# Expert weights in 2 MB pairs: the down pairs issued by ScalarE's queue instead of SyncE's

## What is computed

```python
# grouped_moe, for each of the two layers
scores = sigmoid(t @ router_w)             # 256 tokens x 16 experts
# two experts per token, both inside the best group of four
for e in range(16):
    h = silu(t @ w_gate[e]) * (t @ w_up[e])    # 2048 -> 512, twice
    y = y + combine[:, e:e+1] * (h @ w_down[e])  # 512 -> 2048
x = layer_norm(ALPHA * x + y)
```

## Time and profile before

| | us |
|---|---|
| median of three runs | 1601.77 (1600.47 to 1601.79) |
| profiled execution, its own time | 1603.34 |
| its span, first to last instruction | 1601.4 |
| PE busy | 1539.1 (96%) |
| DVE busy | 699.7 (44%) |
| ACT busy | 453.5 (28%) |
| DMA engines, share of the span that SyncE's queue fills | 79.9% |

### The profile page before, as it was taken

How to read it: one execution, slowest core, us unless ns; L and a number is a source line. 1 busy time by engine, 2 the same in 40 slices (tenths; PEclk the granted TensorE clock), 3 DMA queues, 4 the chain that set the end, 5 groups by cost and what they waited for, 6 DMA issues and landing times.

```text
span 1601.4 us, 18456 instructions
## 1 busy us (share of the span) xinstructions
PE 1539.1 (96%) x7630; PEld 901.7 (56%) x7630; DVE 699.7 (44%) x1010; ACT 453.5 (28%) x600; POOL 9.5 (1%) x19
## 2 busy tenths in 40 slices
PE   9999999999999999899889999999999999999994
PEld 7888887885343343343338888888534335334332
DVE  5544567645333332332247474463543233233325
ACT  5334466434010111011036463342411102111102
POOL 0010000000000000000000000000000000000000
PEclk9999999999999999999999999999999999999998
DMA  8655333578999999999997555457899999999996
GB/s 329 249 194 210 106 132 141 203 280 332 397 428 428 427 427 427 429 426 430 423 414 303 184 200 185 157 203 281 320 424 426 429 426 427 427 428 428 428 422 245
DMA packets 50886, 527.47 MB, mean 329 GB/s; under 512 B 5579, under 2 KB 5643, under 8 KB 12530
## 3 DMA queue, kind: packets, MB, share of 16 engines
q1 hardware_dynamic: 49586, 522.27, 79.9%
q0 software_dynamic: 1216, 4.02, 0.8%
HBM read 524.17 MB, written 2.10 MB: 329 GB/s over the span
## 4 chain that ended last, share of the span: by engine, by line
PE 79%; DMA 16%; DVE 2%; ACT 1%; SPq 1%; issue 0%; DVEq 0%; ACTq 0%
PE bank L1361 29%; DMA w_all<-in_moe_w_down 11%; PE bank L867 10%; PE bank L869 10%; PE bank L868 10%; PE bank L1319 4%; PE bank L1429 3%; DMA router_pair<-in_moe_w_down 2%; DMA w_all<-in_moe_w_gate_up 2%; PE bank L1444 1%; PE bank L1519 1%; DMA w_land<-in_ev_w_in 1%; PE bank L1332 1%; PE bank L1412 1%; PE bank L879 1%; PE bank L931 1%
## 5 line engine op out<-in xcount | busy, mean ns | idle before, releaser
L1361 PE MATMUL bank<-w_all,xg 128*64 128x512 f32 x1856 | 414.4, 596 | 13.1 <-DMA w_all<-in_moe_w_gate_up 11.9
L867 PE MATMUL bank<-w_hi,T_hi 128*128 128x512 f32 x736 | 290.4, 395 | 2.9 <-DVE w_lo L2260 1.4
L869 PE MATMUL bank<-w_hi,T_lo 128*128 128x512 f32 x736 | 286.8, 390 | 0.0
L868 PE MATMUL bank<-w_lo,T_hi 128*128 128x512 f32 x736 | 286.5, 389 | 0.0
L2184 DVE TENSOR_TENSOR w_lo<-w_land,w_hi 128x2048 fp32r<-128x2048 f32 x90 | 205.0, 2289 | 177.6 <-ACT w_hi L1719 177.4
L1361 PEld LDWEIGHTS bank<-w_all,xg 128*64 128x64 f32 x1856 | 127.8, 137 | 268.3 <-issue 241.5
L1719 ACT CAST w_hi<-w_land 128x2048 fp32r<-128x2048 f32 x94 | 178.1, 1911 | 217.9 <-PE bank L869 215.8
L2745 DVE TENSOR_TENSOR y_lo<-bank,y_hi 128x512 fp32r<-128x512 f32 x54 | 37.4, 692 | 415.0 <-ACT y_hi L1980 415.0
L2756 DVE SCALAR_TENSOR_TENSOR X<-bank,weight,X 128x512 f32<-128x512 f32 x224 | 152.5, 744 | 49.6 <-PE bank L1429 49.6
L867 PEld LDWEIGHTS bank<-w_hi,T_hi 128*128 128x128 f32 x736 | 138.2, 188 | 35.2 <-issue 4.3
L869 PEld LDWEIGHTS bank<-w_hi,T_lo 128*128 128x128 f32 x736 | 138.2, 188 | 29.2
(11 more groups left out here) (376 smaller groups left out, 1399.5 us busy)
## 6 DMA issues: line engine op xcount, KB each, us to landing
w_all<-in_moe_w_gate_up SPq DMA_DIRECT2D x114, 2048.0 KB, 20.9
w_all<-in_moe_w_down SPq DMA_DIRECT2D x50, 2048.0 KB, 21.4
w_land<-in_od_w_in SPq DMA_DIRECT2D x32, 1024.0 KB, 4.9
w_land<-in_ev_w_in SPq DMA_DIRECT2D x31, 1024.0 KB, 4.9
router_pair<-in_moe_w_gate_up SPq DMA_DIRECT2D x10, 2048.0 KB, 17.4
w_land<-in_ev_w_out SPq DMA_DIRECT2D x16, 1024.0 KB, 4.8
w_land<-in_od_w_out SPq DMA_DIRECT2D x16, 1024.0 KB, 4.8
router_pair<-in_moe_w_down SPq DMA_DIRECT2D x6, 2048.0 KB, 22.6
```

What stands on the lines that cost most here:

```text
L867: pe.matmul(dst, hi_l, hi_r, start=start, stop=False)
L868: pe.matmul(dst, hi_l, lo_r, start=False, stop=False)
L869: return pe.matmul(dst, lo_l, hi_r, start=False, stop=stop)
L1361: ins = pe.matmul(dst[halves[h], :], cols(c), U.weights(q, pos + h)[:, c, :], start=start and c == 0, stop=stop and c == 3)
```

## The change

ScalarE issues the down pairs. The function `fetch_down(e)` stands in ScalarE's stream right behind `silu(e)` and issues the two down pairs of expert e there (one for expert 0, whose first down pair is among the nine early ones). It waits for the same `used` count as before. In layer 1, from expert 4 on, it reads the expert's number from SBUF, as SyncE did four at a time. SyncE keeps the gate/up pairs, the nine early pairs and the four blocks at the end of a layer. Places, sizes, the order in which TensorE uses the pairs, and all arithmetic stay.

```diff
-                    def down(pos, e):
-                        for p in range(1 if first and e == 0 else 0, 2):
-                            fetch(pos + 2 * p, e, 1, p)
-
                     for e in range(4):
                         up_gate(12 * e, e)
-                        if (e or not first) and not (last and e == 3):
-                            down(12 * e + 8, e - 1)
...
                     def down(pos, e, following):
                         y_out(pos, e, 0)
                         silu(following)
+                        if not (last and following >= 2):
+                            fetch_down(following)
                         if last and following == 2:
                             slots_pair()
                         else:
...
+                    def fetch_down(e):
+                        at_e = 4 * q + e
+                        if layer and at_e >= 4:
+                            act.wait_ge(flag_ready, layer + 1)
+                            number = act.value_load(number_of[0:1, at_e:at_e + 1], min_val=0, max_val=NEXP - 1)
+                        else:
+                            number = at_e
+                        for p in range(1 if at_e == 0 else 0, 2):
+                            n = U.number(q, 12 * e + 20 + 2 * p)
+                            act.wait_ge(used, U.freed(n))
+                            act.dma_start(pair_at(U.place(n)).rearrange("p u n -> p (u n)"),
+                                          moe_src(layer, number, 1, p)).then_inc(pair_in[U.place(n)], 16)
...
                             slots(0)
                             silu(0)
+                            fetch_down(0)
                             continue
```

## The result

The changed kernel takes **1630.74 us** (median of four runs, 1626.64 to 1633.43); the kernel before took 1601.78 beside it (1600.47 to 1603.91). The ratio is 1.0175 with a 95% interval of 1.0163 to 1.0187: slower by 29 us, between 26 and 30. The forecast was 1628, the range 1611 to 1643. The profiled execution of after took 1633.43 us with a span of 1631.5, against 1603.34 and 1601.4.

What follows compares the result with a forecast made beforehand. The prediction took DMA transfers at 428 GB/s, slower than PE, to bound the experts; terms A to D, 12.4 + 8.6 + 3.5 + 1.7 = 26.2 us, added to the 1601.77 median gave 1628 us, range 1611 to 1643.

Steps and rivals of the forecast that it cites:

- What bounds the kernel, and what is removed: Expert stages: transfers at 428 GB/s are slower than PE; no gate/up pair can start earlier, so the gain is zero at best.
- ScalarE's cost at 0: Behind silu: the added issues and read, 0.7 to 1.5 us per expert, are hidden and cost 0.
- Term A: Start of each layer: down pairs issued later leave DMA engines idle, 6.2 us a layer, 12.4 in all.
- No further idle: After a layer's start: later down pairs are delayed less, other transfers stay in flight, so no more DMA time is lost.
- Term B: End of each layer: down pairs overtake the last gate/up pairs, so PE ends it 4.3 us later, 8.6 in all.
- Term C: Layer 1's wide expert 8: PE's release comes later relative to the transfers, 3.5 us of idle DMA; bounds 0 and 6.4.
- Term D: Last wait of each layer: TensorE's clock falls to half behind longer PE waits; one fall, 1.7 us, bounds 0 to 3.4.
- Service transfer by transfer: Rival on both queues: served in order of issue, nothing overtakes and only the layer-start loss stays, 1614 us; 15%.
- a loss or a gain of rate: Two rivals while both queues are active: they move less together, 1635 to 1647 us, 13%; or more, 1598 us, 6%.
- longer and rarer: Sign to look for: PE's waits for gate/up pairs become longer and fewer, in front of j = 2 and 3.

Runs made afterwards that it cites:

- e5: Against the kernel before: SyncE still issues every pair, but each down pair waits for its expert's silu, placed in PE's order of use; 1617.22 us.
- e6: Changed kernel with down pairs of experts 0, 1 and 13 of both layers, and 5 and 6 of layer 1, back on SyncE's queue; 1604.54 us.
- e9: The changed kernel measured once more, without an edit, for a comparison on one chip; 1630.31 us.
- e8: Changed kernel with only the down pairs of experts 5 and 6 of layer 1, ahead of the wide expert, back on SyncE's queue; 1625.92 us.
- e3: Changed kernel with the down pairs of experts 0 and 1 of each layer back on SyncE, issued as early as before; 1622.95 us.
- e10: Changed kernel with eight filler matmuls of 128 x 256 ahead of the fourth gate/up pair of expert 14; 1627.52 us.

## Why the prediction was right, step by step

**What bounds the kernel, and what is removed: held.** SyncE's first gate/up issue behind the nine early pairs stands at 390.57 in after and at 390.35 in the earlier trace rows. Counted from layer 0's first gather, its 65 gate/up issues come 0.0 to 15.9 us later than before, none earlier; no gate/up pair gained from the freed queue. The sentence of the Trainium skill that the prediction set against the change, on the page "DMA: Bandwidth & Descriptors", section "Issuing engines are not separate DMA queues", agrees with the plateaus at 427 to 428 GB/s. About half of the loss was made by the order of landing: e5, with the lateness alone, is 15.1 us over before, after 29.0.

**ScalarE's cost at 0: held where it was looked for.** Two issues take 0.8 us behind silu, and e6, with 20 experts' issues still on ScalarE, is 2.4 us over before in all, which bounds it.

**Term A: 6.2 us a layer, measured 6.4 in layer 0.** The gap at 386 is there, the issue at 410, and the short gap announced for 421 at 422 to 424, where the DMA share is 0.77. The landing of pair 9 was worked out as 423.0 and came at 423.7; PE waited 1.0 us for it, where I had allowed 0.5. By bytes the first 60 us lose 6.4 us. e5 gives 7.4 and 7.3, counted from PE's first release in a layer. "No further idle" from expert 2 on didn't hold where the start was mended: e6 loses 1.1 us a layer there.

**Term B: 4.3 us a layer, measured 4.0.** That is the 9.4 of the tails without a clock fall, less 5.5. Its parts held as well: from the landing of j = 3 PE takes 1608.45 - 1559.19 = 49.3 us in e9's layer 1, as worked out from the earlier trace rows, and j = 3 and the second down pair land 0.6 us apart, as the earlier trace rows had it for two queues that share. The earlier trace rows was weaker than I read it: another 1 MB, issued at 858.29, stood ahead of that transfer on GpSimd's queue. The sharing by halves is shown by after itself, 2.06 MB beside 1.77.

**Term C: 3.5 us, too small.** e8 gives 5.3 by the landings, of which 4.1 is DMA time lost in the stretch shown; the total fell by 3 to 5 us. My step counted only the idle time. That it is a difference of two latenesses fits the other runs. From layer 1's first gate/up matmul to the release behind the wide expert's first pairs it takes 221.7 us in before, 234.4 in after, 233.2 in e3 and 229.0 in e5: PE is 12.7, 11.5 and 7.3 us late. In e5 the transfers are as late as PE, and the ring doesn't run dry; in e3 the transfers lost nothing at the start, and 8.6 us are lost here. But I had put PE's 13 us together from A and the overtaking. Without A that sum leaves 6.8, and e3 shows 11.5. So the 13 came near to after's 12.7 by luck; how PE's lateness in e3 adds up was not shown.

**Term D: 1.7 us, the step that failed.** I took one short fall for the two layers, since the earlier trace rows showed a loss of 1.7 us. The waits were longer than I had put, 6.14 and 5.53 us in front of the last j = 3, and with both the clock stood at half for 6.83 us, of which 4.8 and 5.6 lay behind the wait's end: 9.45 - 7.02 = 2.4 and 9.83 - 7.02 = 2.8, together 5.2, above my upper bound of 3.4. A fall elsewhere went the other way: before, the clock stood at half in layer 1's first gather and after it did not, which gives back 1.35 us.

**The sum.** 2 x 6.4 + 2 x 4.0 + 5.3 + 5.2 - 1.35 = 30.0, beside 30.1 of span, with A as in layer 0 for both. The forecast's 26.2 was short by C and D; the gather's 1.35 us, which I had not foreseen, hid a part of that. The median, 29 us over before and 27 when taken again, lies below the profiled execution; one reason is that not every execution has both falls, as e9 shows. The layers ended 13 and 30.4 us later in the profiled execution, where I had announced 10 to 12 and 24 to 28. Two ends of my range were added up wrongly: B and C halved give 1622, not 1619, and the upper bounds 1637, not 1638.

**The rivals.** Service transfer by transfer is refuted by the overtaking, a loss or a gain of rate as large as these rivals need by the plateaus, which moved by less than 1%. That waits would be "longer and rarer" was half right: longer, and 13 instead of 11.

**What stays open.** The 1.2 us of C beyond the lost DMA time were not placed, nor was the microsecond a layer by which e5 exceeds A. The price of the clock's falls is read from traces; by total time it isn't settled.

## What to carry to other kernels

With the DMA engines full, a second queue bought no rate here, and it gave up what the single queue had: in before all 206 transfers of expert weights landed in the order of issue. Before moving a transfer to another engine's queue, look where that engine's instruction stream will reach the issue, and which earlier transfers it will overtake; in mid-stage that may be free (of the 2.4 us that 20 experts cost here, 2.2 lie near the start of the layers), while at a stage's start, at a stall of the ring and at its end it was paid in full. Terms that share a slack don't add up: mending the start alone handed part of its gain to the wide expert.

## What the runs showed of the hardware that I had not expected

The granted clock stayed at half for 3.41 us behind some waits and for 6.83 behind others; the two longest in the tails of after, 6.14 and 5.53 us, had the long kind. That isn't a matter of length alone: in e8 a wait of 5.52 us from 546.0 had the short kind and one of 5.53 us from 1544.9 the long one. The clock also fell behind waits of 2.49 us (e10) and 2.19 us:

```profile
1550.67 5.35 PE L1355 MATMUL bank<-w_all,xg 128*64 128x512 f32 x16 [2.19 <-DMA w_all<-in_moe_w_gate_up]
1559.23 1.08 PE L1355 MATMUL bank<-w_all,xg 128*64 128x512 f32 x4 [3.21 <-DMA w_all<-in_moe_w_gate_up]
```

This is e9's layer 1: the pair behind the shorter wait takes 5.35 us, at half clock for most of it, and the next, behind 3.21 us of waiting, runs at 1.00 from its start. So the length of one wait doesn't tell whether the pair behind it runs slowly.
